# One DMA per step and direction, no transfers for absent steps, and a gated result in the last layer of a two-layer mixture-of-experts kernel

## What is computed

```python
def _moe(h, gates, w1, w3, w2):
    y = jnp.zeros_like(h)
    for e in range(N_EXPERTS):
        a = jax.nn.silu(h @ w1[e]) * (h @ w3[e])
        y = y + gates[..., e:e + 1].astype(h.dtype) * (a @ w2[e])
    return y
...
        hx = _modulate(x, sh2, sc2)
        yx = _moe(hx, _route(hx, w_router, router_bias), moe_w1[l], moe_w3[l], moe_w2[l])
        x = _layernorm(DEEPNORM_ALPHA * x + g2 * yx, ln_g[l, 1], ln_b[l, 1])
```

## Time and profile before

| | |
|---|---|
| median of three runs | 1207.4 us |
| the profiled execution, its own time | 1211.17 us |
| its span in the profile | 1209.6 us |
| TensorE busy | 992.6 us (82%) |
| VectorE, ScalarE, GpSimd busy | 27%, 19%, 21% |
| expert phase of layer 0, about | 357 to 687 us |
| expert phase of layer 1, about | 930 to 1173 us |
| DMA | 331.42 MB, mean 274 GB/s |

### The profile page before, as it was taken

How to read it: one execution, slowest core, us unless ns; L and a number is a source line. 1 busy time by engine, 2 the same in 40 slices (tenths; PEclk the granted TensorE clock), 3 DMA queues, 4 the chain that set the end, 5 groups by cost and what they waited for, 6 DMA issues and landing times.

```text
span 1209.6 us, 23988 instructions
## 1 busy us (share of the span) xinstructions
PE 992.6 (82%) x9029; PEld 556.0 (46%) x9030; DVE 326.2 (27%) x766; ACT 226.8 (19%) x556; POOL 258.3 (21%) x483
## 2 busy tenths in 40 slices
PE   3999999999999889988885539999989778757860
PEld 1444645564665545544442314545646434423430
DVE  1003033633345212221211256024333312111115
ACT  1311112750231111111100123113513001000000
POOL 0200000010035434442332330000101324311431
PEclk9899999989889999999998959999997879978995
DMA  9995475480354784589999947537574999999942
GB/s 337 364 408 205 148 270 198 150 347 35 139 217 161 283 332 146 204 316 361 390 391 398 389 160 262 198 125 279 220 306 167 398 398 394 400 405 407 393 152 104
DMA packets 89125, 331.42 MB, mean 274 GB/s; under 512 B 10796, under 2 KB 13052, under 8 KB 64500
## 3 DMA queue, kind: packets, MB, share of 16 engines
q1 hardware_dynamic: 66516, 282.13, 60.9%
q0 software_dynamic: 21088, 47.48, 11.2%
q10 hardware_dynamic: 1472, 1.12, 0.3%
HBM read 303.18 MB, written 27.53 MB: 273 GB/s over the span
## 4 chain that ended last, share of the span: by engine, by line
PE 72%; DMA 13%; issue 7%; DVE 4%; ACT 1%; SPq 1%; POOL 1%; POOLq 0%; DVEq 0%; ACTq 0%
PE PS L1802 19%; PE PS L1562 16%; PE PS L1817 8%; PE PS L1724 7%; DMA W<-in_moe_w 6%; DMA XT<-in_moe_w 5%; PE PS L1495 3%; PE PS L1791 3%; PE PS L1528 3%; PE PS L1578 3%; PE PS L1809 2%; DMA W<-in_w_ada 2%; PE PS L1674 1%; PE PS L1686 1%; PE PS L1771 1%
## 5 line engine op out<-in xcount | busy, mean ns | idle before, releaser
L1802 PE MATMUL PS<-W,EX 128*32 128x256 f32 x2912 | 181.0, 399 | 49.6 <-issue 28.3
L1562 PE MATMUL PS<-W,XT 128*128 128x512 f32 (+1 forms) x480 | 190.0, 556 | 2.4 <-ACT XT L797 2.4
L1802 PEld LDWEIGHTS PS<-W,EX 128*32 128x32 f32 x2912 | 96.0, 115 | 117.8 <-issue 66.4
L1562 PEld LDWEIGHTS PS<-W,XT 128*128 128x128 f32 x480 | 91.5, 192 | 96.1 <-issue 93.8
L772 ACT ACTIVATE AT<-EX 64x512 f32<-64x512 f32 x64 | 40.4, 631 | 399.0 <-PE PS L1791 372.9
L670 POOL TENSOR_TENSOR RSTD<-VAR,HALF 128x1 f32<-128x1 f32 (+1 forms) x24 | 16.4, 684 | 458.7 <-DVE VAR L1076 458.7
L1802 PE MATMUL PS<-RAB,EX 128*32 128x256 f32 x640 | 84.3, 423 | 28.9 <-DMA XT<-in_moe_w 16.1
L1366 DVE COPY EX<-PS 128x256 f32<-128x256 f32 x66 | 28.0, 424 | 292.5 <-PE PS L1802 292.5
L701 POOL DMA_DIRECT2D y_rows<-AT x136 | 67.4, 497 | 171.5 <-DVE AT L1376 161.7
L701 POOL DMA_DIRECT2D y_rows<-EX x128 | 63.5, 496 | 152.8 <-DVE EX L1376 138.7
L1817 PE MATMUL PS<-W,AT 128*32 128x256 f32 x1472 | 91.8, 391 | 1.5 <-DVE AT L1373 1.5
(11 more groups left out here) (206 smaller groups left out, 1071.1 us busy)
## 6 DMA issues: line engine op xcount, KB each, us to landing
W<-in_moe_w SPq DMA_DIRECT2D x65, 2048.0 KB, 19.0
W<-in_w_ada SPq DMA_DIRECT2D x24, 2048.0 KB, 12.2
RAB<-in_moe_w SPq DMA_DIRECT2D x10, 2048.0 KB, 19.7
XT<-in_moe_w SPq DMA_DIRECT2D x10, 2048.0 KB, 22.2
H<-in_moe_w SPq DMA_DIRECT2D x10, 2048.0 KB, 16.9
W<-in_w_in SPq DMA_DIRECT2D x7, 2048.0 KB, 21.4
EX<-xg_rows POOLq DMA_DIRECT2D x136, 64.0 KB, 5.7
W<-in_w_out SPq DMA_DIRECT2D x4, 2048.0 KB, 18.8
```

What stands on the lines that cost most here:

```text
L1562: mm = pe.matmul(ps[:, 0:cw], XT[:, k, P * t:P * t + P], w[:, k, :], start=(k == 0), stop=(k == KD - 1))
L1802: mm = pe.matmul(UP_PS[o:o + ROWS, 0:256], rows, w[:, 256 * a:256 * a + 256], start=(k == 0), stop=(k == KD - 1), tile_position=(0, o))
```

## The change

Four edits:

1. `load_rows` and `store_rows` are one DMA each. The DRAM side of the load is now an access pattern of 2 x 32 x 512 elements against 64 partitions of 512, that of the store 4 x 32 x 256 against 128 partitions of 256.
2. Loads of steps that do not exist are not issued (`If(total > n + 4)`), and ScalarE does not stage them (`If(total > n + 2)`, else it only counts up `rows_staged`). The waits on `rows_in` at the layer's end fall away, and that on `rows_staged` comes first.
3. In the last layer the gate vector is laid out for the four groups of 32 partitions (`GQ`, 128 x 256), and `copy_out` multiplies the step's result by it while it leaves PSUM.
4. In the last layer VectorE alone mixes: each gathered row times its weight is added to `X` as soon as that row's own semaphore (`g_last`) says it landed. Both tiles are mixed before either is normalised. `weigh` is gone there.

```diff
+        GQ = RC[:, 1024:1280]
+        g_last = [[sem(f"g_last{t}_{k}") for k in range(2)] for t in range(2)]
...
                 def load_rows(n, b):
-                    for q in range(2):
-                        pool.dma_start(XRAW[b][ROWS * q:ROWS * q + ROWS, :], part_of_rows(xg_rows, n, slice(512 * q, 512 * q + 512)))                            .then_inc(rows_in[b][L], 16)
+                    pool.dma_start(XRAW[b], part_of_rows(xg_rows, n, slice(0, D)).rearrange("s (q d) -> q s d", q=2))\
+                        .then_inc(rows_in[b][L], 16)
                 def store_rows(n, b):
-                    for q in range(4):
-                        pool.dma_start(part_of_rows(y_rows, n, slice(256 * q, 256 * q + 256)), YO[b][ROWS * q:ROWS * q + ROWS, :])                            .then_inc(y_written[b][L], 16)
+                    pool.dma_start(part_of_rows(y_rows, n, slice(0, D)).rearrange("s (q d) -> q s d", q=4), YO[b])\
+                        .then_inc(y_written[b][L], 16)
...
                         with pool.If(total > n):
-                            wait_apart(pool, rows_staged[L], n + 3)
-                            load_rows(n + 4, (3 + c) % 2)
+                            with pool.If(total > n + 4):
+                                wait_apart(pool, rows_staged[L], n + 3)
+                                load_rows(n + 4, (3 + c) % 2)
+                            with pool.Else():
+                                pool.nop()
                             wait_apart(pool, out_copied[L], n + 2)
                             store_rows(n, (3 + c) % 2)
...
+                wait_apart(pool, rows_staged[L], total + 2)
                 for b, half in enumerate(steps_by_half(pool, L)):
-                    wait_apart(pool, y_written[b][L], half * 64)
-                    wait_apart(pool, rows_in[b][L], half * 32 + 32 * b)
-                wait_apart(pool, rows_staged[L], total + 2)
+                    wait_apart(pool, y_written[b][L], half * 16)
...
-                            .then_inc(g_in[t % 2], 16)
+                            .then_inc(g_in[t % 2] if L + 1 < DEPTH else g_last[t][k], 16)
...
-                gates(L, [10, 11])
+                if L + 1 < DEPTH:
+                    gates(L, [10, 11])
+                else:
+                    copy(GQ, full(act, ("gq", L))[:, 0:256], freed(("gq", L)))
...
-                            act.wait_ge(rows_turned[L], n + 2)
-                            wait_apart(act, rows_in[1 - c % 2][L], i * 64 + (c // 2 + 1) * 32)
-                            stage(1 - c % 2)
+                            wait_apart(act, rows_turned[L], n + 2)
+                            with act.If(total > n + 2):
+                                wait_apart(act, rows_in[1 - c % 2][L], i * 32 + (c // 2 + 1) * 16)
+                                stage(1 - c % 2)
+                            with act.Else():
+                                act.sem_inc(rows_staged[L], 1)
                             act.wait_ge(act_turned[L], n + 1)
                             gate()
...
-            for t in range(2):
-                weigh(DEPTH - 1, t)
...
                 def copy_out(b):
-                    dve.tensor_copy(YO[b], DOWN_PS[:, 0:256]).then_inc(out_copied[L], 1)
+                    if L + 1 < DEPTH:
+                        dve.tensor_copy(YO[b], DOWN_PS[:, 0:256]).then_inc(out_copied[L], 1)
+                    else:
+                        dve.tensor_tensor(YO[b], DOWN_PS[:, 0:256], GQ, ALU.mult).then_inc(out_copied[L], 1)
...
                 def mix(t):
+                    if L + 1 == DEPTH:
+                        for k in range(2):
+                            dve.wait_ge(g_last[t][k], 16)
+                            link(dve.scalar_tensor_tensor(out=X[:, t, :], in0=G2[:, t, k, :], scalar=WK2[:, t, k:k + 1],
+                                                          in1=X[:, t, :], op0=ALU.mult, op1=ALU.add))
+                        stats(L, "ln2", t)
+                        return
...
                 for t in range(T):
                     mix(t)
-                    normalise(L, "ln2", t, S["ln2_norm"])
+                    if L + 1 < DEPTH:
+                        normalise(L, "ln2", t, S["ln2_norm"])
+                if L + 1 == DEPTH:
+                    for t in range(T):
+                        normalise(L, "ln2", t, S["ln2_norm"])
...
+                    ps, done = claim(("gq", L))
+                    for m in range(2):
+                        for q in range(4):
+                            mm = pe.matmul(ps[ROWS * q:ROWS * q + ROWS, P * m:P * m + P],
+                                           GATC[:, 1, 2 * q + m, 0:1].to_broadcast([P, ROWS]), IDENT,
+                                           start=True, stop=True, tile_position=(0, ROWS * q))
+                    mm.then_inc(done, 1)
```

More of the change, by code:

```diff
@@ L172, in plan_layer @@
     jobs += [("hx", L, t, hf) for t in range(T) for hf in range(2)]
-    jobs += [("ct", L), ("rk", L)] + mod_jobs(L, 10) + mod_jobs(L, 11)
+    jobs += [("ct", L), ("rk", L)] + (mod_jobs(L, 10) + mod_jobs(L, 11) if L + 1 < DEPTH else [("gq", L)])
     for n in range(3):
@@ L1375, in copy_out @@
                 def copy_out(b):
-                    dve.tensor_copy(YO[b], DOWN_PS[:, 0:256]).then_inc(out_copied[L], 1)
+                    if L + 1 < DEPTH:
[3 more added lines that the diff above has]
+                if L + 1 == DEPTH:
+                    read(dve, ("gq", L))
                 dve.sem_inc(out_copied[L], 1)
@@ L1397, in last_out @@
                         dve.wait_ge(down_done[L], n)
-                        wait_apart(dve, y_written[c % 2][L], i * 128 + (c // 2 + 1) * 64)
+                        wait_apart(dve, y_written[c % 2][L], i * 32 + (c // 2 + 1) * 16)
                         copy_out(c % 2)
@@ L1426, in _ @@
                     lam(L + 1)
-                for c_ in (10, 11):
+                for c_ in (10, 11) if L + 1 < DEPTH else ():
                     for r in mod_streams(L, c_):
@@ L1762, in _ @@
                 mm.then_inc(done, 1)
-                spread(L, 10)
-                spread(L, 11)
+                if L + 1 < DEPTH:
+                    spread(L, 10)
+                    spread(L, 11)
+                else:
+                    ps, done = claim(("gq", L))
[5 more added lines that the diff above has]
+                    mm.then_inc(done, 1)
                 def collect(n):
```

## The result

The changed kernel takes **1228.9 us** (median of four runs, 1227.25 to 1230.96) beside 1207.5 us for the kernel before on the same chip: a ratio of 1.0178 (95% interval 1.0159 to 1.0197), 21 us slower. The forecast was 1195.4, with a range of 1191.5 to 1205.0.

What follows compares the result with a forecast made beforehand. It took TensorE to bound the front of layer 1, the weight stream its expert phase, and serial chains the layer ends. Gains of 2.8 + 2.3 + 6.2 + 0.2 + 0.5 = 12.0 us gave 1195.4 us, range 1191.5 to 1205.

Steps and rivals of the forecast that it cites:

- the landing under edit 1: End of layer 0: the merged 128 KB store lands in 5.5 us, judged by size from 32, 64 and 512 KB transfers.
- the term for the stream: Weight stream in the expert phases: fewer packets from the merged transfers win 0.5 us in all (0 to 2).
- Rival 1: Merged transfers use 2 and 4 DMA engines; layer 0's end loses 2.3 us, layer 1's wins nothing: 1203.3 us, chance 20%.
- Rival 2: Expert phases: narrow loads land in 14.8 us, too late for steps; 8 us lost against Rival 1: 1211.3 us, chance 12%.
- The end of layer 0: From last copy-out to first gather: one store, no absent load ahead, fewer waits; gather starts 2.8 us earlier.
- Edit 4: Final mixing and normalising in layer 1 on VectorE alone: 6.2 us less, bounds 5.5 and 6.5.
- Edit 3's product from PSUM: Copy-out in the last layer: multiplying 256 columns costs 0.425 us, the same as the copy, so nothing lost.
- The end of layer 1: From last copy-out to first gather: store lands in 2.9 us, gather 2.3 us earlier, bounds 0.7 and 2.9.
- Edit 3's 0.2: Start of layer 1's expert phase: shorter gate matmuls win 0.2 us (0 to 0.8), limited by the selection matrix.

Runs made afterwards that it cites:

- e7: e1 with one store DMA a step, 128 x 256 on both sides, which leaves pieces out of order (timing only): 1193.2 us, ratio 0.9874.
- e5: e1 with one load DMA a step, 64 x 512 on both sides, order put right by the copy after the transpose: 1196.3 us, ratio 0.9919.
- e1: The changed kernel with two loads and four stores a step again as before, all its other edits kept: 1195.3 us, ratio 0.9908.
- e9: e2 with four row buffers instead of two and each load issued two steps earlier: 1219.3 us, ratio 1.0087.
- e10: e5 with four row buffers instead of two and each load issued two steps earlier: 1194.5 us, ratio 0.9901.
- e2: e1 with the changed kernel's single merged load DMA, stores still four: 1226.1 us, ratio 1.0166.
- e3: e1 with the changed kernel's single merged store DMA, loads still two: 1206.7 us, ratio 0.9992.
- e8: e1 with transfers for absent steps issued again and the waits at the layer's end as before: 1199.3 us, ratio 0.9929.
- e4: The kernel before with loads and stores each merged into the changed kernel's single DMA, no other edit: 1236.5 us, ratio 1.0242.
- e11: e5 with the single store of e7, which again leaves pieces out of order: 1194.9 us, ratio 0.9890.
- e14: e5 plus an extra 120 KB DRAM-to-DRAM transfer a step, first dimension 2, in runs of 60 KB: 1279.9 us, ratio 1.0607.
- e13: e5 plus an extra 120 KB DRAM-to-DRAM transfer a step, first dimension 2, in pieces of 2 KB: 1232.5 us, ratio 1.0207.
- e12: e5 plus an extra 120 KB DRAM-to-DRAM transfer a step, spread as 7.5 KB for each of 16 engines: 1208.7 us, ratio 1.0016.
- e6: e1 with two store DMAs of 64 KB a step, first dimension 2, instead of four: 1214.4 us, ratio 1.0065.

## Why the prediction was wrong

**The step that failed** is the landing under edit 1: "By size it is nearest to the first two: I take 5.5 us". It took the price of a transfer from its bytes alone and left the pattern to a rival. For a wide transfer that price is nearly right (e7's last store of layer 0 lands in 5.06 us, e5's loads in 6.1); for the narrow ones of edit 1 it is not. And the term for the stream, "I take 0.5 in all (0 to 2)", was a gain from half the packets where the runs show the main loss. Measured: a load of 15.4 us and a store of 9.4 under the stream, 34112 packets for 21088, 373 GB/s for 400, and a loss of 33.6 us (the changed kernel less e1).

**Rival 1 had the mechanism and the wrong place for most of its price.** The packet counts fit 2 and 4 engines. It priced only the two ends of layers, at 5.1 and 2.3 us against the forecast. There the narrow store costs 0.9 and 2.0 us beside e7's wide one: it lands in 5.79 and 4.23 us, where the DMA share is 0.81 and 0.12 (697 to 706 and 1198 to 1206 us) and not 1.02. Of the stream it said "With the stream's gain gone", and so took for a lost gain of 0.5 us what was the largest loss, some 25 us for the loads alone (e9 less e10). The sum had no term for what a narrow transfer does to the transfers beside it.

**Rival 2 named late rows** and set 13 us of landing as the point from which they decide, 14.8 as the landing and 8 us as the price over rival 1. The landing was 15.4, and the late rows cost 5 to 9 us (e2 less e9). This held. The sign came out as in this rival, but its 1211.3 us lacks the stream too. The chain shows where the late rows stand (start us, us, what), all nine at least 15 us long:

```profile
394.97 18.12 DMA EX<-xg_rows
...
570.16 19.06 DMA EX<-xg_rows
590.73 16.30 DMA EX<-xg_rows
608.54 17.70 DMA EX<-xg_rows
...
967.99 15.75 DMA EX<-xg_rows
985.23 24.58 DMA EX<-xg_rows
1011.37 16.90 DMA EX<-xg_rows
...
1142.50 18.30 DMA EX<-xg_rows
1162.27 17.32 DMA EX<-xg_rows
```

**What was right.** The end of layer 0: 2.6 us won for 2.8 (the store's record 0.87 us after the end of the copy-out, landing 5.79, gather 1.05 behind it). Edit 4: 6.4 for 6.2. Edit 3's product from PSUM takes 425 ns, as interpolated in the earlier trace rows. **The end of layer 1** was mis-sized: 1.1 for 2.3. I had 2.9 us for the landing, within a bound of 3.9, and it took 4.23, so that even the bound was too low. This is the narrow cut again: the wide store of e7 lands there in 2.0 us, and the part is 3.1, more than the forecast and than its bound of 2.9. With four small stores (e1) it is 1.3, since the fourth is issued only 1.8 us after the first.

**Edit 3's 0.2** is not visible: the gate's matmuls take 1.08 us instead of 3.35, but the phase then waits 1.26 for the selection matrix. And the 16 matmuls behind it take 6.02 us where they took 3.90, 2.1 us that the prediction had no term for: between 929 and 940 us the granted clock is 0.71, while in the kernel before it is 0.87 between 921 and 932, where TensorE is busy without a gap. e1, e3, e5 and e8 have the same 5.8 to 6.0 us, and e4, without edit 3, has 3.87. Whether it costs the whole kernel anything is not shown. The pass for the variance's power on GpSimd, 0.58 us before, takes 1.55 beside VectorE's passes, and is covered by them.

**As to the size of what was left out:** with the landing as forecast, that is without the narrow cut, the kernel comes to 1195.3 (e1), 1194.5 (e10) and 1196.3 us (e5), where the forecast was 1195.4. Most of it comes from the ends of the layers: 2.1, 1.3 and 6.3 us in e1, and 3.5, 3.0 and 6.3 in e11, where load and store are one wide DMA each and 2.8, 2.3 and 6.2 were forecast. That the forecast of the whole falls on e1's median is in part luck, since e1 has none of the merging and its parts differ from the forecast's. The forecast's 0.5 for fewer packets is not seen in e5, e10 or e11. The version to keep is e1, or e5 or e10 where one load a step is wanted; the three are not told apart. No run has a wide store that keeps the order of the pieces.

**What stays open** is why a weight packet takes longer while two engines are loaded. In e2 q1 needs 91.2% of the engines for 48.25 MB, in e1 92.2% for 51.22. If two burdened engines held up the other 14, that would show as idle engines. e14 has idle time of this kind (share 0.98), but in e2 the share stays at 1.02 and the packets themselves are longer. Whether the 8-byte packets do this is not settled by the records either: in e2 the weight packets that begin in the same quarter of a microsecond as one of them take a median of 336 ns and the others 313, but in e13 both take 316. No run here separates the time of a packet from its wait behind others.

## What to carry to other kernels

When DMAs are merged, look at the first dimension of both access patterns first: by the packet counts a rearrangement that puts a 2 or a 4 in front concentrates the transfer on as many engines, and the same merge with 64 or 128 in front costs nothing. Such a merge changes which piece lies in which partition; the load of e5 is put right by a copy that was there anyway, the store of e7 is not. Read the price in the stretch that the streams bound (GB/s at a DMA share of 1.0) and in the packets of the queue, not only in the landing time of the transfer itself: most of the loss fell on transfers that had not been touched, the weights and the neighbours in GpSimd's queue. To price such a transfer by an added one, as in e12 to e14, look also at what waits for it at the end and whether the loss is longer packets or idle engines. And a rival that has the mechanism is worth as much as the list of places where it is priced; go through every stretch in which the operation runs.

## What the runs showed of the hardware

- A narrow transfer on GpSimd's queue comes with short packets: 224 of 8 bytes for a load with 2 in front (e2), 96 of 16 bytes for a store with 4 in front (the changed kernel). The counts fit as many for each engine that carries nothing as a busy engine has data packets. A load of 128 KB has 272 packets so, and 48 when wide (e5: 20576 - 3840 + 60 x 48 = 19616, as in its profile).
- A spread transfer beside the stream costs less than its bytes at the stream's rate: 8.1 MB more in e12 over both layers cost 12.4 us, some 4.5 of them in the waits at the layers' ends, while at 400 GB/s they would take 20. The same bytes with 2 in front cost 36.2 and 83.6 us.
- A narrow transfer makes other transfers of the same queue land late: the unchanged loads of 64 KB take 8.3 us beside the narrow store of e3 and 10.5 beside those of e6, 5.7 in e1.
- One wide DMA of 128 KB lands within 0.4 us of one of 64 or 32 KB: 6.1 us for 5.7 (load), 5.5 for 5.1 (store), and 2.0 for 1.7 at the quiet end of layer 1 (store). The wide store brings the gather forward by 1.4 us at the end of layer 0 and by 1.8 at that of layer 1 (e7 beside e1); in the whole time this is not told from the noise (1193.2 and 1195.3 us).
- GpSimd's issue takes 651 ns for the narrow load and 707 for the narrow store (medians), 520 for the wide load (e5) and 571 for the wide store (e7), and 496 for each of the small ones.
- Less work for TensorE does not always end sooner: behind the short gate matmuls of edit 3 and the wait after them, the same 16 matmuls take 5.8 to 6.0 us, at a granted clock of 0.68 to 0.71 over the 11 us around them (the changed kernel, e1, e3, e5, e8). Without edit 3 they take 3.9 us at 0.86 to 0.87 (the kernel before, e4).
